# A decoder step on one Trainium2 core: the last sample's values and output projection are moved ahead of the last routers, one logits bank is added, and the bias products are padded and put in a stage of their own

## The reference

```python
q, k, v, u = _project(x, pos, norm1_w, w_in, q_norm_w, k_norm_w)
attn = _diff_head_out(_diff_attn(q, k_all, v_all, lam), subln_w)      # softmax 1 - lam * softmax 2
conv = _conv_mixer(u_ext, conv_w, conv_b, ln_g, ln_b)                 # causal depthwise conv, LayerNorm, swish
x = x + concat([attn, conv]) @ w_out                                  # output projection
h = rmsnorm(x, norm2_w)
logits = h @ router_w + router_b                                      # 32 experts
top_vals, top_idx = top_k(logits, 4); gates = softmax(top_vals)
# each expert: act(h @ w_gate_up[e] + b_gate_up[e]) @ w_down[e] + b_down[e], weighted by its gate
y = x + sum over the four chosen experts
```

## Time and profile before

| what | value |
|---|---|
| median of 3 runs | 1727.53 us (1723.46 to 1727.85) |
| the profiled execution's own time | 1725.22 us, its span 1723.5 us |
| PE busy | 1471.9 us (85%), granted clock 0.905 on average |
| DVE busy | 773.2 us (45%) |
| ACT busy | 355.5 us (21%) |
| DMA | 598.10 MB, mean 347 GB/s |

### The profile page before, as it was taken

How to read it: one execution, slowest core, us unless ns; L and a number is a source line. 1 busy time by engine, 2 the same in 40 slices (tenths; PEclk the granted TensorE clock), 3 DMA queues, 4 the chain that set the end, 5 groups by cost and what they waited for, 6 DMA issues and landing times.

```text
span 1723.5 us, 32057 instructions
## 1 busy us (share of the span) xinstructions
PE 1471.9 (85%) x11950; PEld 591.5 (34%) x11951; DVE 773.2 (45%) x1120; ACT 355.5 (21%) x822; POOL 96.5 (6%) x173
## 2 busy tenths in 40 slices
PE   3878886778887969899998998898999899999970
PEld 2433333345433344332332332332332232332320
DVE  2789878987886244131232132132132131131326
ACT  3212212222222111121212122112122121121220
POOL 0000011000000000000000000000000000000000
PEclk8989995679898858999999998999999999998995
DMA  9557888989998685598999999999999999999986
GB/s 328 183 189 243 296 285 275 359 296 307 313 296 287 233 338 212 228 428 339 424 423 399 417 429 379 411 427 394 402 430 412 398 427 400 410 428 385 429 367 254
DMA packets 127292, 598.10 MB, mean 347 GB/s; under 512 B 20503, under 2 KB 20517, under 8 KB 102026
## 3 DMA queue, kind: packets, MB, share of 16 engines
q1 hardware_dynamic: 109088, 560.20, 82.3%
q10 hardware_dynamic: 8634, 20.00, 3.4%
q0 software_dynamic: 9504, 17.06, 2.6%
HBM read 589.36 MB, written 25.87 MB: 357 GB/s over the span
## 4 chain that ended last, share of the span: by engine, by line
PE 41%; DMA 20%; issue 1%; SPq 0%; DVE 0%; ACT 0%; ACTq 0%; DVEq 0%
PE pair L1517 25%; DMA wts<-in_w_gate_up 16%; PE bank L1554 8%; PE bank L1536 4%; DMA wts<-in_w_down 3%; DMA wts<-y_rows 1%; PE bank L1507 1%; PE bank L1624 1%; PE bank L1565 1%; PE bank L1605 0%; DVE v_ring L2148 0%; DMA h_tok<-h_rows,v_tok 0%; ACT k_T L1161 0%; SPq L646 0%; SPq L657 0%
## 5 line engine op out<-in xcount | busy, mean ns | idle before, releaser
L1517 PE MATMUL pair<-wts,h_T 128*32 128x512 f32 x4032 | 443.9, 597 | 9.6 <-DMA wts<-in_w_gate_up 5.0
L2070 DVE TENSOR_SCALAR q_T<-pair 128x512 f32<-128x512 f32 x32 | 22.1, 692 | 638.9 <-PE pair L1517 638.9
L1517 PEld LDWEIGHTS pair<-wts,h_T 128*32 128x32 f32 x4032 | 129.6, 111 | 307.9 <-issue 297.1
L1554 PE MATMUL bank<-wts,k_T 128*32 128x512 f32 x2048 | 228.3, 596 | 6.4 <-issue 4.9
L1536 PE MATMUL bank<-wts,h_T 128*32 128x512 f32 x992 | 133.1, 676 | 54.4 <-DMA wts<-in_w_gate_up 52.6
L1664 DVE TENSOR_TENSOR wts<-wts,q_b 128x1024 f32<-128x1024 f32 x128 | 158.0, 1234 | 23.3 <-DMA wts<-in_cache_k 17.6
L1667 DVE TENSOR_REDUCE sc<-wts 128x16 f32<-128x1024 f32 x128 | 156.2, 1220 | 4.4
L1151 ACT ACTIVATE h_T<-bank 128x512 f32<-128x512 f32 x66 | 35.9, 595 | 575.8 <-PE bank L1507 575.8
L1554 PEld LDWEIGHTS bank<-wts,k_T 128*32 128x32 f32 x2048 | 65.9, 110 | 146.3 <-issue 137.8
L1229 PE MATMUL pair<-wts,h_T 128*8 128x128 f32 (+1 forms) x480 | 96.0, 476 | 12.1 <-ACT h_T L860 6.4
L1161 ACT ACTIVATE k_T<-bank 32x256 f32<-32x256 f32 x256 | 95.7, 374 | 13.6 <-PE bank L1554 10.2
(11 more groups left out here) (333 smaller groups left out, 1411.0 us busy)
## 6 DMA issues: line engine op xcount, KB each, us to landing
wts<-in_w_gate_up SPq DMA_DIRECT2D x126, 2048.0 KB, 15.7
wts<-in_w_down SPq DMA_DIRECT2D x64, 2048.0 KB, 18.2
wts<-in_cache_k SPq DMA_DIRECT2D x256, 256.0 KB, 3.8
v_ring<-in_cache_v SPq DMA_DIRECT2D x160, 256.0 KB, 3.8
wts<-in_cache_v SPq DMA_DIRECT2D x96, 256.0 KB, 3.9
wts<-in_w_in SPq DMA_DIRECT2D x5, 2048.0 KB, 24.1
wts<-y_rows SPq DMA_DIRECT2D x4, 2048.0 KB, 15.1
wts<-in_w_out ACTq DMA_DIRECT2D x8, 512.0 KB, 6.6
```

The lines of the kernel that those rows point to most:

```text
L1517: m = nc.tensor.matmul(PS[part][p0:p0 + 32, :], lhs[:, 32 * b:32 * b + 32], rhs[:, part * F + half * 512:part * F + half * 512 + 512], sta ...
L1554: m = nc.tensor.matmul(PS[4][p0:p0 + 32, :], act_T[0][:, k, a0:a0 + 32], chunk[c][:, k, n * 512:(n + 1) * 512], start=(c == 0 and k == 0), ...
```

## The change

1. The order. Sample 7's value steps are dealt out two by two from tile 2's router on, so that they end before the last half of tile 4's output projection and before stage 3 of tile 3's router. Behind them come the last sample's steps (`("O", 0)`), the last stage of `("W", 4)`, and `("W", 0)`, with tile 3's stages between them. Then the routers of tile 4 and of the samples are run in turns.
2. The router has seven stages: the slot table stays in stage 5, the bias products, their addition and the store of the residual rows are stage 6.
3. The logits of tile 4 and of the samples (`u` 3 and 4) go to bank `U`, which is free when the last sample's sums have been copied. They wait for that copy and for the reading of the logits before. The wait for `entry_summed` moves to stage 4.
4. The bias products take all 128 rows of both operands: the gates stand in 128 columns (`gsum_pad`, in `u_tok`), of which 96 are zero, and rows 32 to 127 of `bd_pad` are zero. Three more memsets on POOL write the zeros. The transposed gates fill 128 partitions. Tile 4's have a buffer of their own, in `us`.

```diff
-        g_T = k_T[0:E, 0, 256:384]
-        gsum = k_T[:, 0, 480:480 + E]
+        g_T = [us[:, 0:P] if u == TILES - 1 else k_T[:, 0, 256:384] for u in range(TILES + 1)]
+        gsum_pad = u_tok[:, 0:P]
+        gsum = gsum_pad[:, 0:E]
...
-        bd = q_T[0:E, 0:2, :].rearrange("p a n -> p (a n)")
+        bd_pad = q_T[:, 0:2, :].rearrange("p a n -> p (a n)")
+        bd = bd_pad[0:E, :]
...
-        for s in range(1, 3):
-            for n in range(4):
-                plan(("R", s), 1, values=1)
-                plan(("W", s + 1), 1, values=1)
-                if s == 2 and n:
-                    plan(("B", 0), 0)
-            plan(("R", s), 1, 1, values=1)
         for n in range(4):
-            plan(("R", 3), 0, values=2)
-            plan(("W", 4), 0, values=2)
+            plan(("R", 1), 1, values=1)
+            plan(("W", 2), 1, values=1)
+        plan(("R", 1), 1, 1, values=1)
+        plan(("R", 1), 0)
+        for n in range(4):
+            plan(("R", 2), 1, values=1 if n < 2 else 2)
+            plan(("W", 3), 1, values=1 if n < 2 else 2)
+            if n:
+                plan(("B", 0), 0)
+        plan(("R", 2), 0, 0, values=2)
+        plan(("R", 2), 0)
+        plan(("W", 4), 0, values=2)
+        plan(("R", 3), 0, values=2)
+        plan(("W", 4), 0, values=2)
+        plan(("R", 3), 0, 0, values=2)
+        plan(("W", 4), 0, values=2)
         SCHEDULE.append((None, ALL, ALL))
-        plan(("R", 4), 0)
-        plan(("O", 0), 0, 0)
-        plan(("R", 3), 0)
-        plan(("R", 4), 0)
-        plan(("O", 0), 0, 0, 0)
-        plan(("R", 3), 0)
-        plan(("R", 4), 0)
-        plan(("O", 0), 0, 0)
-        plan(("W", 0), 0, 0)
-        plan(("R", 4), 0)
-        plan(("W", 0), 0, 0)
-        plan(("R", 4), 0)
-        plan(("R", 0), 0)
-        plan(("R", 4), 0)
-        plan(("R", 0), *[0] * 5)
+        for part in (("O", 0), ("R", 3), ("O", 0), ("O", 0), ("R", 3), ("O", 0), ("O", 0), ("O", 0), ("W", 4), ("O", 0),
+                     ("W", 0), ("R", 4), ("W", 0), ("W", 0), ("W", 0), ("R", 3), ("R", 4), ("R", 0), ("R", 4),
+                     ("R", 0), ("R", 4), ("R", 0), ("R", 4), ("R", 0), ("R", 3), ("R", 4), ("R", 0), ("R", 4),
+                     ("R", 0), ("R", 0)):
+            plan(part, 0)
...
-                "W": {0: "A", 2: "A"}, "R": {1: "TT", 5: "AA"}, "O": {}, "B": {}}
+                "W": {0: "A", 2: "A"}, "R": {1: "TT", 6: "AA"}, "O": {}, "B": {}}
...
+        def logits_bank(u):
+            return U if u >= TILES - 1 else M
...
+            V.link(nc.gpsimd.memset(gsum_pad, 0.0))
+            V.link(nc.gpsimd.memset(bd_pad[32:64, :], 0.0))
+            V.link(nc.gpsimd.memset(bd_pad[64:128, :], 0.0))
...
-                after(pe, entry_summed, u)
+                if logits_bank(u) is M:
+                    after(pe, entry_summed, u)
+                else:
+                    pe.wait_ge(us_done, NB)
+                    pe.wait_ge(logit_read, u)
...
-                pe.transpose(M[0:E, 320:320 + n], gsum[0:n, :], ident[0:n, 0:n]).then_inc(gT_done, 1)
+                pe.transpose(M[:, 320:320 + n], gsum_pad[0:n, :], ident[0:n, 0:n]).then_inc(gT_done, 1)
...
                 m.then_inc(slot_part, 1)
+                yield
...
-                    nc.tensor.matmul(A[k % 2][0:n, :], g_T[:, 0:n], bd[:, c * 512:(c + 1) * 512],
+                    nc.tensor.matmul(A[k % 2][0:n, :], g_T[u][:, 0:n], bd_pad[:, c * 512:(c + 1) * 512],
...
-                nc.vector.tensor_copy(g_T[:, 0:n], M[0:E, 320:320 + n]).then_inc(gT_copied, 1)
+                nc.vector.tensor_copy(g_T[u][:, 0:n], M[:, 320:320 + n]).then_inc(gT_copied, 1)
```

More of the change, by code:

```diff
@@ L705, in _ @@
             pool.wait_ge(v_out, 16 * TILES)
+            pool.wait_ge(u_out, 32)
+            k, n = filled(t_full, t_no[("P", TILES)][-1])
+            pool.wait_ge(k, n)
+            V.link(nc.gpsimd.memset(gsum_pad, 0.0))
+            V.link(nc.gpsimd.memset(bd_pad[32:64, :], 0.0))
+            V.link(nc.gpsimd.memset(bd_pad[64:128, :], 0.0))
             V.link(pool.iota(iota_e[:, :], [[1, E]], base=0, channel_multiplier=0,
@@ L1400, in part_r @@
                 for kt in range(KT):
-                    m = nc.tensor.matmul(M[0:n, 256:256 + E], h_T[:, kt, 0:n], r_w[:, kt, :],
+                    m = nc.tensor.matmul(logits_bank(u)[0:n, 256:256 + E], h_T[:, kt, 0:n], r_w[:, kt, :],
                                          start=(kt == 0), stop=(kt == KT - 1))
@@ L1892, in part_r @@
                 dve.wait_ge(logits_done, u + 1)
-                add(logit[0:n, :], M[0:n, 256:256 + E], r_b[0:n, :]).then_inc(logit_read, 1)
+                add(logit[0:n, :], logits_bank(u)[0:n, 256:256 + E], r_b[0:n, :]).then_inc(logit_read, 1)
                 dve.wait_ge(logit_read, u + 1)
@@ L1907, in part_r @@
                            gates[0:n, u, :].unsqueeze(2).to_broadcast([n, TOPK, E])))
+                after(dve, gT_done, u)
                 total(gsum[0:n, :], gtmp[0:n, :, :].rearrange("p k e -> p e k")).then_inc(gate_done, 1)
```

## The result

The change made the kernel slower, by a quarter of a per cent: 1728.86 us (median of 20 runs) against 1725.38 us for the kernel before (20 runs beside them), a ratio of 1.0025 with a 95% interval of 1.0014 to 1.0037. The prediction was 1723.8 us and a slight gain. The profiled execution has a span of 1725.9 us; before it was 1723.5.

What follows compares the result with a forecast made beforehand. Expert weight loads bound the kernel but restart with PE, so earlier first tables shift the end in full. Tables 2.8 us earlier gave 1722.4 profiled, 1724.7 off the median; forecast 1723.8, range 1715 to 1731.

Steps and rivals of the forecast that it cites:

- the first term: Stretch from 541.1 us to the last values: sample 7's values moved earlier, ending at 594.5 instead of 597.8.
- The two other waits: Before the last values, PE waits about 1 us for tile 2's exponential and about 5 for sample 6's sums.
- The last sample and both projections: After the last values: `mix` ready by 601, W(0) done at 608.3, 11 us won up to the samples' normalising.
- The new wait: Samples' normalising on ACT waits 8.5 to 9.6 us for tile 4's row store, starting at 618.5, not 610.7.
- Rivals A: Tile 4's row store is quick, landing by 613; tables at about 634, 8.5 us won, 1717 us; chance 0.12.
- C: Tile 4's row store lands behind SP's loads, after 21.3 us; tables at 652, 1736 us; chance 0.13.
- Both routers in turns: From the samples' normalising to the first tables, routers of tile 4 and samples take 21.1 us; tables at 639.6.
- A shift reaches the end in full: At the experts' start: loads restart when PE starts, so any shift of the first expert fully moves the end.
- Theory 3: From the experiments, not the prediction: loads set the end, and a shift of the first expert doesn't reach it.
- Padding: Bias products of 128 rows: height costs nothing, a clock gain of 0 to 4 us is held as nothing.
- B: The clock stays at 1.00 through the last samples and routers; tables about 635.5, 7 us won, 1718.5; chance 0.22.
- D: The order only moves waits: last values at 598, tables at 642 to 644, 1727 to 1729 us; chance 0.13.

Runs made afterwards that it cites:

- e6: The changed kernel with SP's first 2 MB weight load held until tile 2's residual store had landed; ratio 0.9981 to the kernel before.
- e10: The changed kernel with sample 7's values at their old places, tile 4's projection finished before them, new order behind; ratio 0.9949 to the kernel before.
- e7: The changed kernel with SP's first weight load held for tile 2's residual store and an own buffer for the samples' normalised rows; ratio 0.9950 to the kernel before.
- e11: The kernel of e10 with an own buffer for the samples' normalised rows; ratio 0.9909 to the kernel before, 1710.86 us.
- e2: The changed kernel with the samples' 8 normalised rows written to a buffer of their own; ratio 0.9985 to the kernel before.
- e8: The changed kernel with SP's chunks 3 and 2 and all loads behind them held until tile 4's row store had landed; ratio 1.0022 to the kernel before.
- e4: The changed kernel without the padding, its bias products of 32 rows as before; ratio 1.0039 to the kernel before.
- e1: The changed kernel with tile 3's normalising one place earlier, ahead of stage 0 of W(4); ratio 0.9980 to the kernel before.
- e5: The kernel before with the padding of the bias products alone, in the old order; ratio 0.9969 to the kernel before.

## Why the prediction was wrong

The kernel got slower where a slight gain was forecast, by one step of the first term. The terms behind it held to about a microsecond each.

- *"I take 594.5 as tile 3's rows may come a little late: their normalising now stands on ACT behind a wait for tile 2's stored residual."* This is the step that failed. The wait was seen and priced at 0.4 us. The last values end at 601.0, 6.5 us later, and 6.9 us behind the 594.1 of the sum: 5.7 of it is idle time (11.7 us, 6.0 predicted), and 1.3 is PE's busy time (48.3 against 47.0). The store took 10.4 us because the first weight load was already in flight. The prediction worked out just this for the second store and did not ask what SP would have issued by the time of the first. e6 shows the cause and its size: one load held back gives 0.44%. e10, which has the old order there, is 0.76% under the changed kernel. The rest, about 0.3%, is not the store's: e7 against e11, both without a store wait, shows 0.4%. The two other waits, 1 and 5 us, were right: PE idles 1.2 and 5.1 us there.
- *The last sample and both projections.* W(0) ends 13.9 us after the last values, predicted 13.8; `mix` is ready at 607.8, 6.8 after them, predicted about 6.5.
- *The new wait.* Predicted 8.5 to 9.6 us from issue to normalising, measured 10.4. e2 takes the wait away, e8 the slowness of the store: the mechanism is shown. Rivals A (a quick store) and C (21.3 us) fall with it.
- *Both routers in turns.* Predicted 21.1 us, measured 20.5. (At full clock the steps as listed, 17.2, 1 and 1.4, add up to 19.6 and not 19.8; it changes the middle by 0.1.)
- *From the tables to the first expert.* Predicted unchanged at 9.5, measured 10.2; 0.5 of the difference is the gather, 4.89 against 4.40.
- *A shift reaches the end in full.* From the first expert to the end are 1069.7 to 1076.0 us in all fourteen profiles, while the first expert starts between 637.4 and 661.7: Theory 3 falls. The changed kernel has the shortest of these, so its profiled span shows 2.4 us of the 4.3; the medians show 3.5.
- *Padding.* Height costs nothing: right. *"I hold it as nothing in the sum beyond the middle above"*: too low. Full speed comes earlier behind tile 2's products, and the padding is worth 0.31% in the old order. It may have hidden a part of the loss: the reordering without it is 1.0039 (e4), with an interval that overlaps the changed kernel's.
- *Of the rivals,* B's clock did not hold: W(4)'s last quarter ran at 0.50 at first. D, named as an order that only moves waits, came nearest: its time of 1727 to 1729 holds the measured one, but by another way, since it did not name the first store and had the tables at 642 to 644, not 646.

With the sum's own numbers and only the first term put right, the tables come 3.7 us late instead of 2.8 early, and the profiled time would have been 1728.9: within 1.3 of what the spans add up to (1725.9 and the 1.7 us that lie around a span).

## What to carry to other kernels

Before you move a stage, list what is issued in the same microseconds by every other queue in the new order. Moving work earlier also lets the queue behind it go earlier, and a small store can then find itself beside bulk loads and take two to four times as long. A buffer guard that waits for such a store is cheap to remove: a place to write 8 rows was worth 0.4% here, in the changed kernel (e2) and again behind the old head (e11 against e10).

A wait in an in-order queue is best removed at its source. Moving one instruction in front of it (e1) hands a part of the wait to the next; letting the transfer finish sooner (e6) or giving it nothing to guard (e2) removes it.

When a bundle is slower, run its halves. The new order behind the values with a buffer of its own was good for 0.6% beside the padding alone (e11 against e5); without the buffer it is 0.2% (e10 against e5), where the intervals overlap. The new places of the values cost 0.76% (the changed kernel against e10).

## What the runs showed of the hardware

A 512 KB store from ACT's queue took 10.1 to 12.2 us beside 2 MB loads of SP's queue (both stores of the changed kernel 10.4, e1's first 12.2) and 2.7 to 4.6 us without them (before 2.9, e8 2.7, e6 4.6 beside the last loads of cached pages). In the changed kernel the queues from 618.3 to 625.2 us (q1 SP, q10 ACT) read as in the earlier trace rows:

```profile
q1 hardware_dynamic: 167, 2.47, 86.0%
q10 hardware_dynamic: 137, 0.50, 17.6%
```

The packet counts are again nearly equal, and SP's packets are four times as large, so the store gets under a fifth of the time. An indirect gather fared alike: 11.6 us beside the loads (e8), 4.3 to 5.1 in the thirteen other profiles.

Matmuls over 128 rows, of which 96 hold zeros, took as long as over 32 rows (3.76 us for four records against 3.78). Behind tile 2's products full speed came under 2 us later in e5, and 9 us later in the kernel before, where PE was busy throughout; behind tile 3's both stayed at 0.50 up to W(0). No run here tells apart which property of the padded products does this, or why it did it in one place only.
